# Attention's suffix sums as rounded and remainder products in fp32r

## The reference, cut to what matters

```python
z = jnp.einsum('bhqd,bhkd->bhqk', qblk, kh).astype(jnp.float32)
mask = s_idx < t_idx
log_fail = jnp.where(mask, jax.nn.log_sigmoid(-z), 0.0)
tail = lax.cumsum(log_fail, axis=3, reverse=True) - log_fail
log_a = jax.nn.log_sigmoid(z) + tail
a = jnp.where(mask, jnp.exp(log_a), 0.0)
```

## Time and profile before

| | |
|---|---|
| median of 3 runs | 2978.03 us (2976.89 to 2980.73) |
| the profiled execution, its own time | 2978.98 us |
| its span | 2977.3 us |
| TensorE busy | 2328.2 us, 78% |
| VectorE busy | 2038.4 us, 68% |
| ScalarE busy | 1129.9 us, 38% |
| mean granted TensorE clock | 0.88 of full |
| where the change lies | about 1010 to 1142 us of the span |

### The profile page before, as it was taken

The page is one execution under the profiler, slowest core; times in us unless marked ns, Lnnn a source line. Parts: engine busy times, 40 slices in busy tenths (PEclk is TensorE's granted clock), DMA queues, the critical chain, the costliest instruction groups (busy, mean ns, idle before and its releaser), DMA issues.

```text
span 2977.3 us, 28927 instructions
## 1 busy us (share of the span) xinstructions
PE 2328.2 (78%) x10371; PEld 1839.4 (62%) x10371; DVE 2038.4 (68%) x2513; ACT 1129.9 (38%) x1265; POOL 818.7 (27%) x645
## 2 busy tenths in 40 slices
PE   8999999999999999899999990000022249999996
PEld 7888888888888888688888770000011136655663
DVE  5456554554444555745665678999999898887888
ACT  5444344444444554444344342211322244222222
POOL 1000000000000000000000017888887875555553
PEclk9999999999999999999999995555555569999998
DMA  7666556566666546465566559999999967999996
GB/s 268 213 185 197 165 181 189 184 193 190 184 187 185 159 134 206 150 184 170 163 186 225 162 192 396 419 421 414 409 421 405 419 281 306 408 408 394 408 408 274
DMA packets 165304, 792.12 MB, mean 266 GB/s; under 512 B 20189, under 2 KB 20241, under 8 KB 131249
## 3 DMA queue, kind: packets, MB, share of 16 engines
q1 hardware_dynamic: 105344, 390.12, 40.8%
q0 software_dynamic: 59824, 400.23, 33.2%
HBM read 788.17 MB, written 2.10 MB: 265 GB/s over the span
## 4 chain that ended last, share of the span: by engine, by line
PE 59%; DVE 17%; DMA 13%; issue 6%; POOL 3%; ACT 1%; POOLq 0%; SPq 0%; ACTq 0%; DVEq 0%
PE banks L704 52%; DMA v_rows<-in_peer_v_rest,eid 10%; DVE ring L2160 8%; DMA ring<-in_peer_u,eid 3%; DVE banks L2234 2%; POOL ring L634 2%; PE banks L736 1%; PE banks L1079 1%; PE banks L1110 1%; DMA v_raw<-in_peer_v_dense 1%; PE banks L1104 1%; PE banks L716 1%; POOL v_rows L677 1%; DVE onehots L2139 1%; PE banks L784 0%
## 5 line engine op out<-in xcount | busy, mean ns | idle before, releaser
L704 PE MATMUL banks<-w_split,xT 128*128 128x512 f32 x7008 | 1615.9, 392 | 8.0 <-DVE xT L1567 5.4
L704 PEld LDWEIGHTS banks<-w_split,xT 128*128 128x128 f32 x7008 | 1317.7, 189 | 282.9 <-DVE xT L1567 7.1
L1520 DVE TENSOR_TENSOR w_split<-w_raw,w_split 128x1024 fp32r<-128x1024 f32 x592 | 722.3, 1224 | 737.9 <-ACT w_split L1142 736.9
L1142 ACT ACTIVATE w_split<-w_raw 128x1024 fp32r<-128x1024 f32 x592 | 626.1, 1059 | 916.3 <-PE banks L704 878.7
L2160 DVE CUSTOM_DVE_ANT_0 ring<-ring,banks 128x2048 f32<-128x2048 f32 x193 | 436.6, 2284 | 48.3 <-DMA ring<-in_peer_u,eid 45.8
L2234 DVE SCALAR_TENSOR_TENSOR banks<-v_rows,wgt,banks 128x896 f32<-128x896 f32 x254 | 293.0, 1154 | 63.3 <-DMA v_rows<-in_peer_v_rest,eid 60.8
L634 POOL DMA_INDIRECT ring<-in_peer_u,eid x256 | 243.6, 952 | 253.4 <-DVE eid L2092 161.1
L677 POOL DMA_INDIRECT v_rows<-in_peer_v_rest,eid x256 | 247.3, 966 | 233.0 <-DVE banks L2234 194.1
L1110 PE MATMUL banks<-v_raw,wT 128*128 128x512 f32 (+1 forms) x1024 | 299.3, 435 | 0.7 <-ACT wT L1430 0.7
L642 POOL TENSOR_TENSOR ring<-ring,h 128x2048 f32<-128x2048 f32 x63 | 284.7, 4519 | 36.8 <-DMA ring<-in_peer_u,eid 35.5
L568 POOL DMA_DIRECT2D row_a<-in_final_g x1 | 0.5, 534 | 1068.9 <-DVE ao L1782 1068.9
(11 more groups left out here) (318 smaller groups left out, 1321.4 us busy)
## 6 DMA issues: line engine op xcount, KB each, us to landing
w_raw<-in_a_w_in SPq DMA_DIRECT2D x192, 512.0 KB, 3.5
v_raw<-in_peer_v_dense SPq DMA_DIRECT2D x128, 576.0 KB, 8.1
w_raw<-in_b_w_in SPq DMA_DIRECT2D x128, 512.0 KB, 3.6
w_raw<-in_w_in SPq DMA_DIRECT2D x112, 512.0 KB, 3.6
w_raw<-in_a_w_out SPq DMA_DIRECT2D x64, 512.0 KB, 4.5
w_raw<-in_b_w_out SPq DMA_DIRECT2D x32, 512.0 KB, 4.5
w_raw<-in_w_out SPq DMA_DIRECT2D x32, 512.0 KB, 4.5
w_raw<-in_peer_wq SPq DMA_DIRECT2D x32, 512.0 KB, 3.8
```

The source lines that it names most:

```text
L704: last = mm(ps[half][:, 2 * t + n, :], xt[:, xp, kk, tok], w_split[:, s, wp, n * BANK:(n + 1) * BANK], start=(k == 0 and xp == 0 and wp == ...
L1142: fn(w_split[:, k % SPLIT_SLOTS, 0, :], w_raw[:, k % RAW_SLOTS, :], ACT.Copy).then_inc(hi_done, 1)
L1520: v.tensor_tensor(w_split[:, s, 1, :], w_raw[:, k % RAW_SLOTS, :], w_split[:, s, 0, :].bitcast(F32), ALU.subtract).then_inc(split_done, 1)
```

## The change

The suffix sums are computed from the softplus in two parts, rounded to fp32r and the remainder, with the triangle and the ones in fp32r too (exact there). New are:

- `att_constants` on ScalarE, first job of `att_z0` behind step 0: two copies of 128x128 to fp32r.
- `att_hi(g)` on ScalarE: waits for the masked softplus, copies 128x1536 to `sp_hi` (one buffer for all groups, so group g also waits until unit `L{g-1}` is filled). It stands ahead of the copy of Z1 for g = 0, and behind steps 6, 14 (of `att_z0`) and 6 (of `att_z1`) for the others.
- `att_lo(g)` on VectorE: softplus minus `sp_hi`, 128x1536, written in the softplus's place. Behind steps 3, 7, 15 and 7.
- `att_l` on TensorE waits for `att_lo`. A head takes four fp32r products in place of three plain ones: 384 and 128 columns with the rounded part, then the same with the remainder.

```diff
             def att_l(g):
-                pe.wait_ge(sp_done, g + 1)
+                pe.wait_ge(sp_lo_done, g + 1)
...
-                    s = sp_[:, g % 2, j, :]
-                    mm(ps[hf][:, j, 0:TOKENS], onward[:, :], s[:, 0:TOKENS], start=True, stop=False)
-                    mm(ps[hf][:, j, P:TOKENS], ones[:, 0:P], s[:, TOKENS:ZW], start=False, stop=True)
-                    last = mm(ps[hf][:, j, TOKENS:ZW], onward[:, :], s[:, TOKENS:ZW], start=True, stop=True)
+                    for n, s in enumerate((sp_hi[:, j, :], sp_lo[:, g % 2, j, :])):
+                        mm(ps[hf][:, j, 0:ZW], onward_r[:, :], s, start=n == 0, stop=False)
+                        last = mm(ps[hf][:, j, P:TOKENS], ones_r[:, :], s[:, TOKENS:ZW], start=False, stop=n == 1)
...
+            def att_constants():
+                is_emptied(act, "qkT3")
+                act.wait_ge(consts_done, 2)
+                fn(onward_r[:, :], onward[:, :], ACT.Copy)
+                fn(ones_r[:, :], ones[:, 0:P], ACT.Copy)
+
+            def att_hi(g):
+                act.wait_ge(sp_done, g + 1)
+                if g:
+                    is_filled(act, f"L{g - 1}")
+                fn(sp_hi[:, :, :], sp_[:, g % 2, :, :], ACT.Copy).then_inc(sp_hi_done, 1)
...
-            block_of("att_z0", at={0: [lambda: att_copy(0)], 1: [lambda: att_ln(0)], 2: [lambda: att_copy(1)],
-                                   3: [lambda: att_ln(1)], 5: [lambda: att_exp(0)], 10: [lambda: att_exp(1)],
-                                   12: [lambda: att_copy(2)], 13: [lambda: att_ln(2)]})
+            block_of("att_z0", at={0: [att_constants, lambda: att_copy(0)], 1: [lambda: att_ln(0)],
+                                   2: [lambda: att_hi(0), lambda: att_copy(1)],
+                                   3: [lambda: att_ln(1)], 5: [lambda: att_exp(0)], 6: [lambda: att_hi(1)],
+                                   10: [lambda: att_exp(1)], 12: [lambda: att_copy(2)], 13: [lambda: att_ln(2)],
+                                   14: [lambda: att_hi(2)]})
...
             block_of("att_z1", at={2: [lambda: att_exp(2)], 4: [lambda: att_copy(3)], 5: [lambda: att_ln(3)],
+                                   6: [lambda: att_hi(3)],
...
+            def att_lo(g):
+
+                dve.wait_ge(sp_hi_done, g + 1)
+                v.tensor_tensor(sp_lo[:, g % 2, :, :], sp_[:, g % 2, :, :], sp_hi[:, :, :].bitcast(F32), ALU.subtract)\
+                    .then_inc(sp_lo_done, 1)
...
-                                   3: [lambda: att_sp(1)], 5: [lambda: att_la(0)], 8: [lambda: att_out(0)],
+                                   3: [lambda: att_lo(0), lambda: att_sp(1)], 5: [lambda: att_la(0)],
+                                   7: [lambda: att_lo(1)], 8: [lambda: att_out(0)],
                                    10: [lambda: att_la(1)], 12: [lambda: att_abs(2)], 13: [lambda: att_sp(2)],
-                                   15: [lambda: att_out(1)]})
+                                   15: [lambda: att_lo(2), lambda: att_out(1)]})
...
-                                   7: [lambda: att_out(2)], 8: [att_gate(0)], 9: [lambda: att_la(3)],
+                                   7: [lambda: att_lo(3), lambda: att_out(2)], 8: [att_gate(0)], 9: [lambda: att_la(3)],
```

More of the change, by code:

```diff
@@ L271, in build @@
         sp_ = sb("softplus", [P, 2, 4, ZW], F32, ROWS + 12 * KB)
+        sp_lo = sb("softplus_lo", [P, 2, 4, ZW], F32R, ROWS + 12 * KB)
+        sp_hi = sb("softplus_hi", [P, 4, ZW], F32R, T1 + 24 * KB)
+        onward_r = sb("onward_r", [P, P], F32R, T1 + 30 * KB)
+        ones_r = sb("ones_r", [P, P], F32R, T1 + 30 * KB + 512)
         row_a = sb("row_a", [P, D], F32, ROWS)
@@ L411, in build @@
         sp_done = sem("sp_done")
+        sp_hi_done = sem("sp_hi_done")
+        sp_lo_done = sem("sp_lo_done")
         la_done = sem("la_done")
```

## The result

The changed kernel took 2986.18 us (median of 6 runs, 2984.68 to 2989.85), the kernel before in the same comparison 2977.46: ratio 1.0024, interval [1.0014, 1.0033], which is 7.1 us more, between 4 and 10. The forecast was +4.2 us, as likeliest case no change beyond 0.2%; the first median lies in the range of 2977 to 2988 but above its likeliest part (2981 to 2985), with a ratio just beyond the 0.2%; the second median, 2982.82, lies in that part.

A forecast was written before the change was run, and what follows sets the result against it. TensorE bounds the stage, with ScalarE and VectorE later at O0 and att_z1. Waits of +2.5, +0.8, +3.7, +0.5 less three savings of 1.2 make +3.9; 0.3 for the clock gives +4.2, 2982.7 us, range 2977 to 2988.

The forecast's parts named there:

- 0.3 for the clock: At att_z1: added for the lower clock holding longer after the 6.3 us wait, estimated at 0 to 1.7 more.
- The products: L units on TensorE: 2.29 us in place of 3.43, saving about 1.2 each; bounds 1.9 and 3.1.
- The copies: att_hi on ScalarE 1.47 us, att_lo on VectorE 1.75; the two constants below 0.8, costed at nothing.
- L0: Ahead of L0: TensorE stands still 4.1 us until att_lo(0), as att_hi(0) holds up the copy of Z1.
- `att_z1`: Ahead of att_z1: TensorE's wait grows from 2.6 to 6.3 us, the Silu being queued behind att_hi(2); +3.7.
- L1's wait of 0.8: Ahead of L1: TensorE, there at 1055.4, waits until 1056.2 for att_out(0) to free half B; +0.8 us.
- The clock at L0: After L0's wait: a clock fall costing 1.7 us, hidden 1.3 at O0 and the rest at L1; nothing on top.
- L3's wait: Ahead of L3 in att_z1: att_lo(3) ends at 1116.45 against L3's start at 1115.95; +0.5 us.
- A saving of 4.7: Rival for the four L units: products' saving rules if att_hi holds up nothing, 2974.3 us; chance 0.05.
- Narrow products that don't get faster: Rival for L units: 128 columns in fp32r cost 0.21 us, a unit saves 0.4; +6.6, 2985.6 us; chance 0.08.
- The clock falls more often: Rival at L0 and att_z1: lower clock lasts twice as long, up to 1.7 us more at each; +6 to +9; chance 0.12.
- Shorter links: Rival for the chains: about ten links each 0.1 us shorter, units of 1.9; together 2.2 less, +2, 2981; chance 0.20.

The follow-up runs named there:

- first profile: The changed kernel as first profiled: stage 136.33 us, against 129.66 for the kernel before; timed median 2986.18 us, ratio 1.0024.
- second profile: The changed kernel again with nothing edited, against the kernel before: median 2982.82 us, ratio 1.0013; stage 134.27 us.
- the products alone: Changed kernel without remainder or hi and lo copies, same 16 fp32r products a unit on the rounded softplus: ratio 0.9994 to the kernel before, stage 127.66 us.
- the copies alone: Changed kernel with both copies and all waits kept, but L multiplying the plain softplus as before: ratio 1.0028 to the kernel before, stage 139.21 us.
- TensorE kept busy: Changed kernel plus 16 products ahead of L0 whose results L0 overwrites: ratio 1.0013 to the kernel before, stage 133.69 us.
- the placed kernel: Changed kernel with only the steps behind which attention's jobs stand altered, on three engines: ratio 0.9965 to the kernel before, stage 121.68 us.
- the same places with plain products: Kernel before with the placed kernel's new places, without copies or fp32r products: ratio 0.9991 to the kernel before, stage 126.36 us.
- the swap: Changed kernel with the copy of Z1 ahead of hi of group 0 on ScalarE: stage 133.65 us, one run, no ratio.
- the three moves: Changed kernel with Z1's copy ahead of group 0's hi, group 2's hi and lo behind the Silu, L3 one step later: ratio 0.9989, stage 127.52 us.
- group 2's copies moved: Changed kernel with hi and lo of group 2 put behind the Silu, in att_z1: ratio 1.0004 to the kernel before, stage 130.13 us.
- L3 moved: Changed kernel with L3 behind step 10 of att_z1 in place of 9: stage 132.41 us, one run, no ratio.

## Why the prediction was right, and where it was off

Its direction and its mechanism were right, but for one queue that it left out (L3) and the length of the clock's fall. In us later than before, measured from Z0:

| start of | predicted | first profile | second profile |
|---|---|---|---|
| L0 | 4.1 | 3.98 | 3.98 |
| O0 | 2.5 | 4.30 | 2.76 |
| L1 | 3.3 | 4.19 | 2.65 |
| Z2 | 2.1 | 2.99 | 1.49 |
| `att_z1` | 5.8 | 6.61 | 5.11 |
| L2 | 5.8 + 0.3 for the clock | 7.34 | 5.28 |
| L3 | 5.4 | 7.79 | 5.73 |
| end of the stage | 4.2 | 6.67 | 4.61 |

- **The products.** 2.29 a unit predicted, 2.23 measured (1.15 and 1.20 saved). A pair of 384 and 128 columns starts every 0.286 us, the term taken; the row of 8 columns in the earlier trace rows was the right neighbour. That L0's saving would count for nothing is shown by the wait at O0 with the products alone, where the clock was up between L0 and O0. In the changed kernel the clock fell there, and the copies alone against the second profile show L0's 1.2 counting.
- **The copies.** `att_hi` 1.49 for 1.47, `att_lo` 1.75 for 1.75, the two constants 0.30 each, in ScalarE's idle time.
- **L0.** Right in place, releaser and size: 3.80 waited, 4.1 predicted.
- **`att_z1`.** Right: 6.21 for 6.3; +3.6 for +3.7.
- **L1's wait of 0.8.** It was not there in either profile of the changed kernel, and was 0.2 with the clock up (TensorE kept busy). I had the emptying of O0 end at 43.7 us from Z0; it ended at 43.0 in both profiles and in that run. The chain up to the Exp of group 0 was 0.3 shorter than my sum, and behind it instructions that I put end to end overlap by 0.1 each, 0.4 in all.
- **The clock at L0.** The loss was to vanish in the waits at O0 and L1. That held in the second profile, where the products from L0 to O0 lost some 1.6 and L1 came 0.13 later than with TensorE kept busy. It failed in the first: the lower clock lasted 6.8 us and not 3.4, the loss was some 3.1, and 1.67 of it was left at L1. The term that was too small is the length of the fall, which I took from the one fall of the kernel before.
- **L3's wait.** The step that failed by omission: 0.5 predicted, 1.66 measured in delay. I had followed `att_lo(3)` but not the queue behind it: L3 needs half B, which `att_out(2)` frees, and that stands behind `att_lo(3)` on VectorE. This costs a further 1.2, the length of that copy. One step later, L3 doesn't wait.
- **Sizes.** Of the 2.5 between 6.67 and 4.2, L3 is 1.2, O0 1.8 (2.0 of the clock, less 0.2 by which the chain was shorter) and the clock at `att_z1` 0.4, less 0.9 at L1 and 0.1 at `att_z1`'s wait. The second profile's 4.61 lies close to the sum in part by chance: the omitted 1.2 and the wait that did not exist offset each other.
- **The rivals.** A saving of 4.7 is what the placed kernel shows against the same places with plain products, so it can be had, but only in another order. Narrow products that don't get faster are excluded by the 2.23. "The clock falls more often" happened in the first profile: 1.8 at O0 as that rival said, but at `att_z1` only 0.7 of its 1.7. Shorter links were there, by 0.2 up to O0 and 0.7 up to the emptying of O0.

Whether the kernel is slower by more than 0.2% stays open: the two comparisons overlap from 1.0014 to 1.0022.

## What to carry to other kernels

A copy that waits for another engine costs what is queued behind it, on an engine that does many jobs; put it where its input is ready, before counting what the products behind it save. When such a job is added, walk the list of everything behind it up to the next unit that TensorE waits for, the emptying of PSUM too: the dearest delay here (3.6 of 6.7) was the Silu behind a copy that it had nothing to do with. And measure a change of a few us by the stage's own marks in the trace, in more than one profile.

## What was not expected of the hardware

The lower clock after a wait is not a fixed price. What the profiles show, by the wait of TensorE ahead of it:

| wait | lower clock |
|---|---|
| 1.95 to 1.96 us | none in both placed kernels and with the swap; 3.4 us with the three moves (0.78 of full over the 7.6 us from 1033.4) |
| 2.52 us | 3.4 us with the products alone, at O0 |
| 2.59 to 2.60 us | 3.4 us in the kernel before, with the products alone and with the three moves; none with group 2's copies moved |
| 3.80 to 3.81 us | 6.8 us in the first profile and with group 2's copies moved; 3.4 us in the second profile, with the copies alone and with L3 moved |
| 6.21 us | 6.8 us in all six profiles that have it, beginning 2.3 to 4.8 us into the wait |

What it costs is what falls on products: between the restart after 6.21 us and L2, 1.4 to 2.5 us were lost, measured against the 8.30 that this takes at full clock. Between two profiles of the same program this alone made 2.1 us, where the change made 6.7 in the one and 4.6 in the other.
